# Selection scratch and search maxima in PSUM, and the softmax joined after 56 expert score blocks instead of 64

## The reference, cut to what matters

```python
q = (xt @ wq).reshape(T, HEADS, 2, 128)
s = einsum('thpd,hpnd->thpn', q, keys)            # 8 heads, 2 halves, 128 keys
v1, i1 = top_k(s[:, :, 0], 16);  v2, i2 = top_k(s[:, :, 1], 16)
sc, ci = top_k(all 256 sums v1 + v2, 16)
e = i1[ci // 16] * 128 + i2[ci % 16]              # row number of the expert, 8 x 16 per token
g = softmax(sc)
out = sum over the 128 chosen experts of g * gelu(x . u_tab[e]) * v_tab[e]
```

## Time and profile before

| | us |
|---|---|
| median of 3 runs (lowest, highest) | 2099.57 (2099.16, 2107.41) |
| the profiled execution | 2090.23 |
| its span, first to last instruction | 2088.4 |
| busy: TensorE 2013.8, weight loads 1872.8, VectorE 1680.2, ScalarE 790.1, GpSimd 926.0 | |
| mean granted TensorE clock | 0.984 of full speed |

### The profile page before, as it was taken

The page is one execution under the profiler, slowest core; times in us unless marked ns, Lnnn a source line. Parts: engine busy times, 40 slices in busy tenths (PEclk is TensorE's granted clock), DMA queues, the critical chain, the costliest instruction groups (busy, mean ns, idle before and its releaser), DMA issues.

```text
span 2088.4 us, 34317 instructions
## 1 busy us (share of the span) xinstructions
PE 2013.8 (96%) x11788; PEld 1872.8 (90%) x11788; DVE 1680.2 (80%) x3320; ACT 790.1 (38%) x1061; POOL 926.0 (44%) x652
## 2 busy tenths in 40 slices
PE   4989998999899999999999999999999999999997
PEld 3989997999799999999899999988999999999987
DVE  5539998442478999995899999977888888888887
ACT  3434655322523332323355555543323333333232
POOL 1222322333122477777666666654333333333341
PEclk9999999999899999999999999999999999999998
DMA  9212212444521389898788888779999999999993
GB/s 381 107 56 62 61 56 71 173 140 162 192 71 62 126 298 307 299 308 301 250 320 327 336 327 334 281 228 363 347 345 354 345 346 398 347 347 353 342 356 139
DMA packets 172455, 523.06 MB, mean 250 GB/s; under 512 B 17616, under 2 KB 71248, under 8 KB 170704
## 3 DMA queue, kind: packets, MB, share of 16 engines
q1 hardware_dynamic: 97776, 267.67, 36.7%
q0 software_dynamic: 55296, 201.35, 26.9%
q10 hardware_dynamic: 19296, 52.96, 6.4%
HBM read 463.71 MB, written 58.20 MB: 250 GB/s over the span
## 4 chain that ended last, share of the span: by engine, by line
PE 73%; DVE 17%; issue 3%; DMA 3%; ACT 2%; POOL 1%; SPq 0%; DVEq 0%; POOLq 0%; ACTq 0%
PE P L843 29%; PE P L569 21%; PE P L754 14%; PE P L778 5%; DVE rows L1530 2%; DVE rowsX L1530 2%; PE P L657 1%; PE P L601 1%; DVE oh L1569 1%; DVE keysel L1573 1%; DVE oh L1562 1%; DMA tb<-in_posT 1%; DMA raw<-in_wblk 1%; PE P L719 1%; DVE cand L1517 1%
## 5 line engine op out<-in xcount | busy, mean ns | idle before, releaser
L867 ACT ACTIVATE wHi<-raw 128x1024 fp32r<-128x1024 f32 x330 | 346.4, 1050 | 1142.8 <-PE P L843 422.3
L511 POOL DMA_INDIRECT rows<-in_v_tab,Eg x192 | 218.2, 1137 | 385.4 <-DVE accB L1688 225.0
L494 POOL TENSOR_TENSOR wLo<-raw,wHi 128x1024 fp32r<-128x1024 f32 x128 | 308.4, 2410 | 176.0 <-ACT wHi L867 173.2
L754 PE MATMUL P<-hHi,wHi 128*128 128x448 f32 x1024 | 381.6, 373 | 5.0 <-POOL wLo L494 5.0
L488 POOL TENSOR_TENSOR wLo<-raw,wHi 128x1024 fp32r<-128x1024 f32 (+1 forms) x76 | 185.6, 2443 | 445.0 <-ACT wHi L867 438.1
L754 PE MATMUL P<-hLo,wHi 128*128 128x448 f32 x1024 | 378.0, 369 | 0.0
L754 PE MATMUL P<-hHi,wLo 128*128 128x448 f32 x1024 | 377.8, 369 | 0.0
L569 PE MATMUL P<-hHi,wHi 128*128 128x320 f32 x960 | 228.8, 319 | 15.1 <-DVE hLo L1274 10.6
L1640 DVE TENSOR_TENSOR wLo<-raw,wHi 128x1024 fp32r<-128x1024 f32 x128 | 156.7, 1225 | 84.1 <-ACT wHi L867 77.9
L569 PE MATMUL P<-hLo,wHi 128*128 128x320 f32 x960 | 220.0, 310 | 0.0
L569 PE MATMUL P<-hHi,wLo 128*128 128x320 f32 x960 | 220.0, 310 | 0.0
(11 more groups left out here) (243 smaller groups left out, 3763.8 us busy)
## 6 DMA issues: line engine op xcount, KB each, us to landing
raw<-in_ublk SPq DMA_DIRECT2D x128, 512.0 KB
raw<-in_v_tab SPq DMA_DIRECT2D x128, 512.0 KB
raw<-in_wblk SPq DMA_DIRECT2D x104, 512.0 KB
gel_scratch<-gel ACTq DMA_DIRECT2D x128, 224.0 KB
gsr<-gel_scratch SPq DMA_DIRECT2D x128, 224.0 KB
gate_scratch<-stage ACTq DMA_DIRECT2D x5, 4096.0 KB
gates4a<-gate_scratch SPq DMA_DIRECT2D x16, 640.0 KB
gates4b<-gate_scratch SPq DMA_DIRECT2D x16, 640.0 KB, 7.0
```

What stands on the lines that cost most here:

```text
L494: pool.tensor_tensor(wLo[:, n % 2, :], raw[:, n % 4, :], wHi[:, n % 2, :].bitcast(f32), ALU.subtract).then_inc(raw_used[n % 4], 1)
L511: pool.indirect_dma_start(out=row(n), out_offset=None, in_=tab, in_offset=bass.IndirectOffsetOnAxis(ap=Eg[:, buf, at:at + 1], axis=0)).the ...
L754: last = nc.tensor.matmul(P[0][:, j % 2, 0:TD], w_[:, j % 2, k * 128:(k + 1) * 128], x_[:, k, C0:T], start=(k == 0 and a == 0 and b == 0), ...
L867: return nc.scalar.activation(out, in_, f, **kw)
```

## The change

1. The scratch of `select` for tiles 1 to 4 (`ab`, `abf`) becomes `abP`, `abfP`, in the first bank of `P[1]`; only the float copy of the candidate positions (`cf`, L1548) stays in SBUF. Tile 0 keeps SBUF.
2. The maxima of the first half (`v16[:, n % 2, 0, :]`) go to `v16P` in the second bank of `P[3]` once `dotted[1]` is above zero; the second half's stay in SBUF.
3. `iotaP` goes; the one-hots compare with `iota16` in SBUF, and ScalarE makes one copy less.
4. U1, U2 = 64, 64 becomes 56, 72. With it the 80 early gathers lie over 48 blocks instead of 56, the 112 late ones over 70 instead of 62, the softmax joins after 56 blocks, and 16 blocks without gates follow the 56 with gates, instead of 8.

```diff
-U1, U2 = 64, 64
+U1, U2 = 56, 72
...
-    iotaP, i1P = P[3][:, 1, 0:16], P[3][:, 1, 16:16 + SLOTS].rearrange("p (a c) -> p a c", a=2)
+    i1P = P[3][:, 1, 16:16 + SLOTS].rearrange("p (a c) -> p a c", a=2)
...
+    v16P = P[3][:, 1, 144 + SLOTS:176 + SLOTS].rearrange("p (n k) -> p n k", n=2)
+    abfP = P[1][:, 0, 0:SLOTS].rearrange("p (a c) -> p a c", a=2)
+    abP = P[1][:, 0, SLOTS:2 * SLOTS].bitcast(u32).rearrange("p (a c) -> p a c", a=2)
...
-        actf(iota128P, iota128[:, :], ACT.Copy)
-        actf(iotaP, iota16[:, :], ACT.Copy).then_inc(s["psum_in"], 1)
+        actf(iota128P, iota128[:, :], ACT.Copy).then_inc(s["psum_in"], 1)
...
-                v, ix = v16[:, n % 2, :, :], i16[:, t % 3, :, h * TOPK:(h + 1) * TOPK]
+                v = (v16P[:, n % 2, :] if dotted[1] else v16[:, n % 2, 0, :], v16[:, n % 2, 1, :])
+                ix = i16[:, t % 3, :, h * TOPK:(h + 1) * TOPK]
...
-                                           v[:, 0, a0:a1].unsqueeze(2).broadcast_to([128, na, bs]),
-                                           v[:, 1, 0:bs].unsqueeze(1).broadcast_to([128, na, bs]), ALU.add)
+                                           v[0][:, a0:a1].unsqueeze(2).broadcast_to([128, na, bs]),
+                                           v[1][:, 0:bs].unsqueeze(1).broadcast_to([128, na, bs]), ALU.add)
...
-            c, abn, abfn, ohn = CI[:, t % 3, h0 * TOPK:h1 * TOPK], ab[:, :, 0:n], abf[:, :, 0:n], oh[:, :, 0:n * TOPK]
-            i1, io = (i1b, iota16[:, :]) if t == 0 else (i1P, iotaP)
+            i1, ab_, abf_ = (i1b, ab, abf) if t == 0 else (i1P, abP, abfP)
+            c, abn, abfn, ohn = CI[:, t % 3, h0 * TOPK:h1 * TOPK], ab_[:, :, 0:n], abf_[:, :, 0:n], oh[:, :, 0:n * TOPK]
+            cf = abf[:, 0, 0:n]
             ch.link(V.tensor_copy(i1[:, :, 0:n], i16[:, t % 3, :, h0 * TOPK:h1 * TOPK]))
-            ch.link(V.tensor_copy(abfn[:, 0, :], c))
+            ch.link(V.tensor_copy(cf, c))
             ch.step(V.tensor_scalar(abn[:, 0, :], c, 3, None, ALU.bitwise_and))
             ch.step(V.tensor_copy(abfn[:, 1, :], abn[:, 0, :]))
-            ch.step(V.tensor_tensor(abfn[:, 1, :], abfn[:, 0, :], abfn[:, 1, :], ALU.subtract))
+            ch.step(V.tensor_tensor(abfn[:, 1, :], cf, abfn[:, 1, :], ALU.subtract))
...
-                                    io.unsqueeze(1).unsqueeze(1).broadcast_to([128, 2, n, TOPK]), ALU.is_equal))
+                                    iota16[:, :].unsqueeze(1).unsqueeze(1).broadcast_to([128, 2, n, TOPK]), ALU.is_equal))
```

More of the change, by code:

```diff
@@ L1478, in place @@
             return SC[:, c:c + 8]
+        dotted = [0, 0]
         def search(n, now, before):
@@ L1485, in search @@
                 h, t = now
-                v, ix = v16[:, n % 2, :, :], i16[:, t % 3, :, h * TOPK:(h + 1) * TOPK]
+                v = (v16P[:, n % 2, :] if dotted[1] else v16[:, n % 2, 0, :], v16[:, n % 2, 1, :])
+                ix = i16[:, t % 3, :, h * TOPK:(h + 1) * TOPK]
                 for p in range(2):
-                    last = V.max(v[:, p, 0:8], scores_of(h, t, p))
+                    last = V.max(v[p][:, 0:8], scores_of(h, t, p))
             if before is not None:
@@ L1495, in search @@
                 for p in range(2):
-                    V.max_index(ix[:, p, 0:8], v[:, p, 0:8], scores_of(h, t, p))
+                    V.max_index(ix[:, p, 0:8], v[p][:, 0:8], scores_of(h, t, p))
                 for p in range(2):
-                    last = V.match_replace(sw[:, p, :], v[:, p, 0:8], scores_of(h, t, p), BIG)
+                    last = V.match_replace(sw[:, p, :], v[p][:, 0:8], scores_of(h, t, p), BIG)
             if before is not None:
@@ L1504, in search @@
                 for p in range(2):
-                    last = V.max(v[:, p, 8:16], sw[:, p, :])
+                    last = V.max(v[p][:, 8:16], sw[:, p, :])
             if before is not None:
@@ L1510, in search @@
                 for p in range(2):
-                    last = V.max_index(ix[:, p, 8:16], v[:, p, 8:16], sw[:, p, :])
+                    last = V.max_index(ix[:, p, 8:16], v[p][:, 8:16], sw[:, p, :])
             if before is not None:
@@ L1532, in dots @@
                                    ).then_inc(s["row_free"], 1)
-        dotted = [0, 0]
         def early_dots(n):
@@ L1544, in select @@
             n = (h1 - h0) * TOPK
-            c, abn, abfn, ohn = CI[:, t % 3, h0 * TOPK:h1 * TOPK], ab[:, :, 0:n], abf[:, :, 0:n], oh[:, :, 0:n * TOPK]
-            i1, io = (i1b, iota16[:, :]) if t == 0 else (i1P, iotaP)
+            i1, ab_, abf_ = (i1b, ab, abf) if t == 0 else (i1P, abP, abfP)
+            c, abn, abfn, ohn = CI[:, t % 3, h0 * TOPK:h1 * TOPK], ab_[:, :, 0:n], abf_[:, :, 0:n], oh[:, :, 0:n * TOPK]
+            cf = abf[:, 0, 0:n]
             ch.link(V.tensor_copy(i1[:, :, 0:n], i16[:, t % 3, :, h0 * TOPK:h1 * TOPK]))
-            ch.link(V.tensor_copy(abfn[:, 0, :], c))
+            ch.link(V.tensor_copy(cf, c))
             ch.step(V.tensor_scalar(abn[:, 0, :], c, 3, None, ALU.bitwise_and))
             ch.step(V.tensor_copy(abfn[:, 1, :], abn[:, 0, :]))
-            ch.step(V.tensor_tensor(abfn[:, 1, :], abfn[:, 0, :], abfn[:, 1, :], ALU.subtract))
+            ch.step(V.tensor_tensor(abfn[:, 1, :], cf, abfn[:, 1, :], ALU.subtract))
             ch.step(V.tensor_scalar(abfn[:, 1, :], abfn[:, 1, :], 3.0, -192.0, ALU.mult, ALU.add))
-            ch.step(V.scalar_tensor_tensor(out=abfn[:, 1, :], in0=abfn[:, 0, :], scalar=64.0, in1=abfn[:, 1, :],
+            ch.step(V.scalar_tensor_tensor(out=abfn[:, 1, :], in0=cf, scalar=64.0, in1=abfn[:, 1, :],
                                            op0=ALU.is_ge, op1=ALU.mult))
-            ch.step(V.tensor_tensor(abn[:, 1, :], abfn[:, 0, :], abfn[:, 1, :], ALU.add))
+            ch.step(V.tensor_tensor(abn[:, 1, :], cf, abfn[:, 1, :], ALU.add))
             early_dots(1)
```

## The result

The changed kernel is slower by 0.3%: 2105.81 us (median of 18 runs, 2098.88 to 2109.65) against 2098.74 us of before in the same comparison (18 runs, 2092.19 to 2107.41), ratio 1.0032, 95% interval 1.0021 to 1.0043, that is 4.4 to 9.0 us. The forecast was 2.2 us slower and no change beyond 0.5%. The mechanism was the forecast one; the term for VectorE's saving was too large.

A forecast was written before the change was run, and what follows sets the result against it. TensorE, busy for 96% of the span, was taken as the bound. First-part dot waits and the longer end gave +6.8 us, less 4.6 at the last gathers, +2.2: 2099.6 to 2101.8 us, range 2093 to 2112.

The forecast's parts named there:

- the term for VectorE's saving: First part: of 20.0 us of collisions removed, 15.6 us were to be saved by the 52nd dot.
- What bounds, and what the change can reach.: TensorE, busy 96% of the span, keeps the same work; the change can only remove or add its few pauses.
- Selection in PSUM.: VectorE's moved small instructions lose 20.0 us of collisions with GpSimd's subtractions; net 18.5 us after the PSUM surcharge.
- The surcharge of 1.5 us: Extra cost of PSUM operands in VectorE's selection: lower bound zero, upper bound 10 us, 1.5 taken.
- "L1548 (5.0 us) still goes from SBUF to SBUF and keeps its collisions.": VectorE's cast of the candidate positions was to stay at 5.0 us, collisions included.
- Rival A: Collisions stay or PSUM costs as much: 9.8 us slower, or 17.7 without any saving; 0.17 for over 10.5 us.
- The dots hold the gathers.: First part: early gathers catch up with VectorE's dots, GpSimd and TensorE stall; block 54 ends at 969.9, sum +6.8 us.
- the signs of being wrong: Block 54 ending near 961 or past 978, small instructions over 0.35 us, or new VectorE landing waits in the longer end.
- The join at no change.: After the score blocks: transposes, copies, six dots and one-hots unchanged, so the wait for the first gates costs the same.
- The second part.: Eight more gateless blocks at the end cost 39.3 us; shorter waits at the last gathers return 4.6 of 5.5 us.
- Rival B: Dots don't hold the gathers, and all 5.5 us at the end go: 2.5 us faster, 2097; chance 0.25.
- rival C: End of the score blocks keeps its loss, landings under DMA load being slower than 8.93 us: +6.8, 2106; chance 0.15.

The follow-up runs named there:

- run 4: The changed kernel with D1 = 72 instead of 80, eight early gathers fewer in the first part; 2090.47 us, ratio 0.9970 against before.
- run 2: The changed kernel with U1, U2 = 64, 64, so only the places in PSUM; 2097.14 us, ratio 1.0000 against before.
- run 3: The changed kernel with the position cast going into PSUM and a copy from there to SBUF; 2095.76 us, ratio 0.9996 against before.
- run 5: The changed kernel with both D1 = 72 and the position cast by way of PSUM; 2092.07 us, ratio 0.9967 against before.
- run 8: The changed kernel with D1 = 72 and the six dots laid behind the first block's one-hots; 2087.69 us, ratio 0.9943 against before.
- run 9: The changed kernel with cast by way of PSUM, U1, U2 = 60, 68, and one-hots ahead of the six dots; 2084.26 us, ratio 0.9936 against before.
- run 10: The kernel before with only the six dots laid behind the first block's one-hots; 2092.00 us, ratio 0.9974 against before.
- run 11: The kernel before with U1, U2 = 56, 72 and D1 = 64, nothing in PSUM; 2094.33 us, ratio 0.9992 against before.
- run 1: The kernel before with U1, U2 = 56, 72 alone, nothing moved to PSUM; 2122.36 us, ratio 1.0129 against before.
- run 7: The kernel before with U1, U2 = 56, 72 and D1 = 72, nothing in PSUM; 2115.67 us, ratio 1.0085 against before.

## Why the prediction held, and where it was off

**What bounds, and what the change can reach.** Right. TensorE's work is the same, and the thirteen kernels differ up to block 127 only in its pauses.

**Selection in PSUM.** The collisions of the moved instructions went as priced: the sums of the earlier trace rows for them fell to 1.4 to 1.8 us for six, 3.3 for sixteen. The surcharge of 1.5 us was right as well; a 64-element cast or tensor_scalar takes 222 to 232 ns in PSUM, some 35 more than undisturbed in SBUF, a 128-element cast 300 instead of 230, and a tensor_tensor 228 instead of 225. The upper bound of 10 us falls with it. The Trainium skill (VectorE: DVE Perf Modes, the section on the TRN2 errata) gives 120 fixed cycles for a PSUM source and 58 for one in SBUF. An estimate from that page, 62 cycles more for a source, gives 8 us for the sum and 0.26 us for such an instruction; the traces don't agree, and the measurement decides.

**"L1548 (5.0 us) still goes from SBUF to SBUF and keeps its collisions."** This is the step that was mis-sized. It did not keep them, it took on others': 10.0 us in the changed kernel, 8.5 with only the places in PSUM. Of the 20.0 us that the moved instructions gave up, 5 came back there. The 51 dots up to the 52nd took 168.7 us instead of 179.6, 10.9 saved where 15.6 were forecast. In run 4, where the cast took 4.7 us, about as before the change (5.0), they took 163.4: 16.2 saved, so the rest of that term was sized rightly. Rival A named this ("a stall removed may reappear at L1548") and its own arithmetic (each missing microsecond delays block 44 by one) fits: forecast for the end of block 54 969.9, measured 978.26 less the 3.13 us of later start, 975.1, that is 5.2 us late. The 52nd dot and the gather of row 59 behind it, from the timelines of VectorE and GpSimd:

```profile
917.64 1.22 DVE L1535 SCALAR_TENSOR_TENSOR rows<-rows,P 128x1024 f32<-128x1024 f32 x1
...
919.67 0.94 POOL L514 DMA_INDIRECT rows<-in_u_tab,Eg  x1 [3.92 <-DVE rows L1535]
```

The dot is over at 918.9, or 915.7 without the later start, where 911.7 was forecast: 4.0 of the 5.2 us. The gather begins 0.8 us behind the dot's end, for which the forecast's chain had nothing. The last 0.4 is one more pause, at block 47.

**The dots hold the gathers.** Right, and shown by runs 2, 3, 4 and 5. Forecast were some 9 us of pauses in blocks 30 to 47, measured 12 in the rows of waits and 14.2 in the rhythm, from block 22 on. One number of that part was wrong without effect: undisturbed, block 44 starts at 906.3, not 911.3 (911.3 is its end); the 969.9 was worked out from 915.4 and stands. The scm_ready of about 947 came at 954, the 68th dot's end at 958.6 instead of 951 and the exponential at 966.8 instead of 957, for the same 5 us and the 3 of the start. Of the signs of being wrong one came by the letter: block 54 ended at 978.26, past the 978 of rival A. Without the later start it is 975.1, between the forecast's 970 and that sign, as the saving was (10.9 us, between 15.6 and rival A's 8).

**The join at no change.** Right for the change (31.2 against 30.6 us). It could be had apart, by the order of the six dots (runs 8 to 10).

**The second part.** 39.3 - 4.6 = 34.7 us were forecast for the longer way from the join to block 127, measured 34.3: the join took 0.6 more, and behind it all 5.5 us of the forecast's list went, not 4.6. The long wait of GpSimd at the gather that opens the last sixteen is gone with the block that it stood in, and the last blocks kept the rhythm of 4.91 us at 325 GB/s (1371.5 to 1444 us). VectorE's waits for landings, named as a sign of being wrong, did grow there, from 19 us (1385 to 1440 us, before) to 43 (1371 to 1446 us), but TensorE was busy all the time.

**The sum.** +6.8 - 4.6 = +2.2 was forecast; with the 5.2 us that block 54 came late, 0.6 of the join and 0.9 more gained at the end it is +7.1, measured +6.6 in the profile and +7.1 in the medians. Rival B (dots don't hold the gathers) fell; rival C (the end keeps its loss) fell.

**What stays open.** Why the cast takes 4.7 us in run 4, 7.0 in run 11 and 8.5 in run 2, none of which has many waits of GpSimd for dots, was not settled; feedback alone doesn't tell it, since the cast of run 2 took over others' collisions without it (four of 1.40 to 2.43 us). Where the cast falls between GpSimd's instructions was not varied by itself, nor the number of gathers per block without the waits.

## What to carry to other kernels

When an idle engine is "early", ask what else its results release besides the wait in view: here VectorE was 20 us early for the softmax and just in time for the row buffers, and it was the second that the shift of eight blocks used up. Two instructions that exclude each other don't lose their collision when one of a row is moved away; the next that can collide inherits part of it, here a quarter (5 of 20 us), so move all of them, as run 3 did, or count on less. And where an engine in a shared order (gather, then low part) waits for the engine it collides with, the wait itself sets the phase and can make the collisions worse: slow the asking down a little, as fewer early gathers did here, before making the answer faster.

## What the runs showed of the hardware that was not expected

A small VectorE instruction on SBUF can be held from before the recorded start of GpSimd's subtraction on. The cast of the changed kernel began at 851.56, within a gather's issue of 851.11 to 852.05, and ended with the subtraction that followed, after 2.95 us; the subtraction itself takes 2.39. The profile of before shows a hold without a subtraction:

```profile
751.30 0.95 POOL L511 DMA_INDIRECT rowsX<-in_u_tab,Eg  x1
...
751.34 0.20 DVE L1550 CAST abf<-ab 128x64 f32<-128x64 uint32 x1
...
751.83 0.43 DVE L1552 TENSOR_SCALAR abf<-abf 128x64 f32<-128x64 f32 x1
```

The cast that begins with the issue takes its undisturbed 0.20 us; the tensor_scalar that begins 0.53 us into it ends with it, after 0.43 us. The small instructions of select that work on SBUF alone and began in the first 0.62 us of a gather's issue (the change and runs 1, 2, 4, 7, 8, 10, 11 and before, 741 to 990 us) follow one pattern:

| began, us into the issue | subtraction directly behind the gather | something else or a gap behind it |
|---|---|---|
| 0 to 0.29 | not held | not held |
| 0.35 to 0.52 | held to the subtraction's end, 2.93 to 3.11 us (10 cases) | not held |
| 0.53 to 0.62 | held to the subtraction's end, 2.82 to 2.91 us (3 cases) | held to the end of the issue, 0.38 to 0.43 us (18 cases) |

The Trainium skill (SBUF — State Buffer, "SBUF: two separate sides") describes the lock between the engines' instructions as held for the whole instruction, and the trace agrees for the subtraction; the issue of a gather held VectorE's instructions in its later part only.

The collisions were larger in the two kernels in which GpSimd waited long for dots: 23.8 us beyond the undisturbed lengths with 3 us of such waits before, 30.3 and 35.3 with 56 and 52 us of them (runs 1 and 7), 22.7 with 9 (run 11). That the waits made all of the difference is not shown, since the gathers per block changed with them.
